# The narrow feed-forward round moved from first to last, with all five wide down projections in seven products

## The reference, cut to what matters

```python
D_FF = ((8 * D_MODEL + 3 * 256 - 1) // (3 * 256)) * 256      # 2816
...
    h2 = rms_norm(x, norm2_g)
    ffn = (jax.nn.silu(h2 @ w_ffn_gate) * (h2 @ w_ffn_up)) @ w_ffn_down
    return x + ffn
...
    for l in range(DEPTH_2):          # 2 layers
        x = hybrid_layer(x, l, ...)
    return rms_norm(x, final_g)
```

## Time and profile before

| | |
|---|---|
| median of 3 runs | 2476.74 us (2476.72 to 2477.36) |
| profiled execution: time / span | 2478.95 / 2477.2 us |
| TensorE busy | 2441.6 us, 99% of the span, 11994 matmuls |
| VectorE busy | 1599.9 us, 65% |
| ScalarE busy | 1143.3 us, 46% |
| GpSimd busy | 196.1 us, 8% |
| granted TensorE clock, mean | 0.998 |

### The profile page before, as it was taken

How to read it: one execution, slowest core, us unless ns; L and a number is a source line. 1 busy time by engine, 2 the same in 40 slices (tenths; PEclk the granted TensorE clock), 3 DMA queues, 4 the chain that set the end, 5 groups by cost and what they waited for, 6 DMA issues and landing times.

```text
span 2477.2 us, 31952 instructions
## 1 busy us (share of the span) xinstructions
PE 2441.6 (99%) x11994; PEld 1984.8 (80%) x11994; DVE 1599.9 (65%) x2918; ACT 1143.3 (46%) x2011; POOL 196.1 (8%) x212
## 2 busy tenths in 40 slices
PE   8999999999999999999999999999999999999998
PEld 7888878788777787888888887887787887888887
DVE  6767668654657677546666686645558686556666
ACT  3437455333745656323333444336647473433333
POOL 0001000100000000002222000000000000022220
PEclk9999999999999999999999999999999999999999
DMA  5321223233323221233333242233233312333331
GB/s 153 87 76 31 86 78 119 61 89 103 85 74 94 88 89 55 72 116 102 102 102 102 61 145 67 71 94 114 60 94 84 88 64 85 98 124 101 96 101 69
DMA packets 118970, 221.70 MB, mean 89 GB/s; under 512 B 14353, under 2 KB 21825, under 8 KB 118305
## 3 DMA queue, kind: packets, MB, share of 16 engines
q1 hardware_dynamic: 114192, 201.60, 26.9%
q0 software_dynamic: 4480, 17.79, 2.5%
q10 hardware_dynamic: 144, 0.26, 0.0%
HBM read 215.40 MB, written 4.23 MB: 89 GB/s over the span
## 4 chain that ended last, share of the span: by engine, by line
PE 91%; DVE 4%; ACT 3%; issue 2%; DMA 0%; SPq 0%; ACTq 0%; DVEq 0%
PE bank L749 52%; PE bank L746 21%; PE bank L805 6%; PE bank L929 2%; PE bank L940 2%; PE bank L1006 1%; PE bank L905 1%; PE bank L906 1%; PE bank L955 1%; PE bank L990 1%; PE bank L1044 1%; PE bank L823 0%; DVE tab L2019 0%; DVE hL L1928 0%; PE bank L837 0%
## 5 line engine op out<-in xcount | busy, mean ns | idle before, releaser
L1825 DVE TENSOR_TENSOR wL<-wraw,wH 128x1024 fp32r<-128x1024 f32 (+2 forms) x356 | 446.3, 1254 | 569.2 <-ACT wH L1223 567.3
L1223 ACT ACTIVATE wH<-wraw 128x1024 fp32r<-128x1024 f32 (+2 forms) x356 | 364.7, 1024 | 859.2 <-PE bank L749 633.2
L749 PE MATMUL bank<-hH,wH 128*128 128x512 f32 x1704 | 686.0, 403 | 1.8 <-ACT hH L1297 0.9
L749 PE MATMUL bank<-hH,wL 128*128 128x512 f32 x1704 | 666.3, 391 | 0.0
L749 PE MATMUL bank<-hL,wH 128*128 128x512 f32 x1704 | 665.8, 391 | 0.0
L749 PEld LDWEIGHTS bank<-hH,wH 128*128 128x128 f32 x1704 | 320.5, 188 | 76.1 <-issue 11.1
L749 PEld LDWEIGHTS bank<-hL,wH 128*128 128x128 f32 x1704 | 320.6, 188 | 72.3 <-issue 7.7
L749 PEld LDWEIGHTS bank<-hH,wL 128*128 128x128 f32 x1704 | 320.3, 188 | 70.1
L746 PE MATMUL bank<-wH,hH 128*128 128x512 f32 (+2 forms) x736 | 281.8, 383 | 0.0
L746 PE MATMUL bank<-wL,hH 128*128 128x512 f32 (+2 forms) x736 | 276.9, 376 | 0.0
L746 PE MATMUL bank<-wH,hL 128*128 128x512 f32 (+2 forms) x736 | 276.8, 376 | 0.0
(11 more groups left out here) (365 smaller groups left out, 3447.6 us busy)
## 6 DMA issues: line engine op xcount, KB each, us to landing
wraw<-in_w_in_dram SPq DMA_DIRECT2D x180, 512.0 KB, 3.6
wraw<-in_w_ffn_gate_dram SPq DMA_DIRECT2D x40, 512.0 KB, 3.7
wraw<-in_w_ffn_up_dram SPq DMA_DIRECT2D x40, 512.0 KB, 3.6
set<-in_w_ffn_down_dram SPq DMA_DIRECT2D x32, 512.0 KB, 6.1
wraw<-in_w_out_dram SPq DMA_DIRECT2D x24, 512.0 KB, 3.5
wraw<-in_w_ffn_down_dram SPq DMA_DIRECT2D x12, 512.0 KB, 3.5
wraw<-in_w_up_a_dram SPq DMA_DIRECT2D x8, 512.0 KB, 3.5
wraw<-in_w_up_b_dram SPq DMA_DIRECT2D x8, 512.0 KB, 3.5
```

What stands on the lines that cost most here:

```text
L749: mm = pe.matmul(bank[b.bank0 + t][:, :], w_part[:, kk, t * P:(t + 1) * P], act_part[:, k, :], start=first, stop=last)
L1223: A(wH[:, u % W_SLOTS, 0:width], wraw[:, u % RAW_SLOTS, 0:width], ACT.Copy).then_inc(S["w_hi"], 1)
L1825: V.tensor_tensor(wL[:, u % W_SLOTS, 0:width], wraw[:, u % RAW_SLOTS, 0:width], wH[:, u % W_SLOTS, 0:width].bitcast(F32), ALU.subtract).th ...
```

## The change

The rounds are now five of 512 features and then one of 256. All five wide ones (0 to 4) have their down projection in seven products, beside the projections of rounds 1 to 5. FU0 uses banks 4 to 7, FU5 banks 2 and 3. FD50 and FD51 have two chunks of hidden features instead of four: FD50 one unit, FD51 two units of one chunk. The last norm's weight on the left halves is multiplied by GpSimd, and ScalarE's left output waits for it (`left_gained`).

```diff
@@ Block.__init__
-            self.units = [(k, 2) for k in order or range(0, kchunks, 2)]
+            width = 1 if by_tile and kchunks == 2 else 2
+            self.units = [(k, width) for k in order or range(0, kchunks, width)]
...
-FFN_COLS = [256] + [512] * 5
-SEVEN = (1, 2, 3, 4)
+FFN_COLS = [512] * 5 + [256]
+SEVEN = (0, 1, 2, 3, 4)
...
-                               bank0=n // P if f == 0 else 0)
+                               bank0=NT if f == 0 else n // P if n < SEQ else 0)
...
@@ gpsimd, behind the last round's sums
+            pool.wait_ge(S["gp_step"], 16 * 6)
+            for t in range(NT):
+                pool.wait_ge(S["half_ready"], 5 * NT + t + 1)
+                pool.tensor_tensor(x[:, t, LEFT], x[:, t, LEFT], final_g[:, LEFT], ALU.mult).then_inc(
+                    S["left_gained"], 1)
...
@@ scalar, left_out(t)
                     act.wait_ge(S["rstd_ready"], 5 * NT + 1 + t + 1)
+                    act.wait_ge(S["left_gained"], t + 1)
...
@@ vector, last_squares
-                    for t in range(NT if gain else 0):
-                        left = x[:, t, 0:SEQ]
-                        V.tensor_tensor(left, left, final_g[:, 0:SEQ], ALU.mult)
```

More of the change, by code:

```diff
@@ L158, in dense_plan @@
     units, groups = [], 0
-    used = [0] * (GATE_BANK + 1)
+    used = [0] * 8
     for b in blocks:
@@ L494, in build @@
         names = """
-            x_tile0 x_tile1 x_tile2 x_tile3 ident_norm consts masks_ready landed0 landed1 landed2 w_hi w_lo groups free0 free1 free2 free3 free4 free5
+            x_tile0 x_tile1 x_tile2 x_tile3 ident_norm consts masks_ready landed0 landed1 landed2 w_hi w_lo groups free0 free1 free2 free3 free4 free5 free6 free7 left_gained
             act_step dve_step gp_step
@@ L510, in build @@
         landed = [S["landed0"], S["landed1"], S["landed2"]]
-        free = [S[f"free{j}"] for j in range(GATE_BANK + 1)]
+        free = [S[f"free{j}"] for j in range(8)]
         block = ctx.enter_context(nc.Block())
@@ L1871, in left_rows, with last_squares @@
                     half_square(t, 0)
-            def last_squares(b, gain):
+            def last_squares(b):
                 def between(i):
@@ L2857, in _ @@
                         last_rows(L, name, right_out if L == DEPTH else xn_rows,
-                                  last_squares(B(ffn_order()[-2])[0], L == DEPTH))
+                                  last_squares(B(ffn_order()[-2])[0]))
                     elif name == ffn_order()[-2]:
```

## The result

The changed kernel took 2488.98 us (median of 6 runs, 2488.18 to 2490.98) against 2477.05 of the kernel before (6 runs, 2476.43 to 2478.57): a ratio of 1.0049, 95% interval 1.0038 to 1.0059, or 11.9 us more. Forecast were 5.7 more. TensorE's count fell as written (11994 to 11970 matmuls), and its share of the chain that ended last fell from 91 to 90%, while VectorE's rose from 4 to 5%.

A forecast was written before the change was run, and what follows sets the result against it. TensorE was taken to bound the kernel (91% of the chain), VectorE its very end. -4.15 + 2 x 1.4 + 3.94 + 3.13 = +5.7 us on 2476.74 gave 2482.5 us, range 2479.2 to 2486.0.

The forecast's parts named there:

- TensorE's count: Feed-forward part, both layers: twelve fewer down-projection matmuls per layer, -2.07 us each, -4.15 in all.
- FG0 and FU0 with 512 columns: First feed-forward round of each layer: starting with 512 columns brings no stall, 0 us.
- Product 0 of the narrow round: FG5/FU5: VectorE's weight subtraction waits for GpSimd's s2, ends behind product 0's due time; 1.4 us stall per layer.
- the worse case: Narrow round: VectorE's subtraction behind a 2.4 us GpSimd operation instead of a 1.29 one, stalling product 0 by 2.5 us.
- The end of layer 1: From FD50 to the next layer's AQ: VectorE's work nearly unchanged, giving back +3.94 us of the 10.88 taken off.
- of layer 2: From FD50 to the kernel's end: VectorE's list and collisions with GpSimd's multiplications give back +3.13 us of 10.88.
- the turn at a square: Layer 2's end: GpSimd's multiplication of row 0 holds VectorE's square of row 1 up by 0.55 us.
- the turn at the first scaling: Layer 2's end: GpSimd's multiplication of row 3 holds VectorE's first final scaling up by 0.4 us.
- Product 2's subtraction: Later in the narrow round: GpSimd's t4 done near 13.4 us, four us before product 2; no stall counted.
- rival 2: Narrow round falls further behind: products 2 and 3 delayed 0.5 to 1 us each, product 0 2.5; 2486, chance 0.10.
- rival 1: Fewer collisions: product 0 waits 0.45 us, last stage has none; +2.9, 2479.6, chance 0.27 including what lies between.

The follow-up runs named there:

- early weights: Changed kernel with product 0's weights in the narrow round FG5 copied by ScalarE and subtracted by VectorE one unit earlier: 2480.43 us, ratio 1.0014.

## Why the prediction was wrong

- *TensorE's count, -4.15*: right. 24 matmuls fewer, and from FG0's plain run to the first products it is 51.7 us in layer 2 where it was 2205.91 - 2121.35 = 84.6: 32.8 less, forecast 32.64.
- *FG0 and FU0 with 512 columns, 0*: right. That run stands in the chain without a break.
- *Product 0 of the narrow round, +1.4 a layer*: this is the step that failed. It measured 3.2. The mechanism, turns with GpSimd, was right, and I had a price for the worse case: "with a 2.4 us GpSimd operation in front instead of a 1.29, 2.5". But I took the order of two instructions from a schedule in which they stood 0.1 us apart, and treated it as given. They came 0.04 us apart, the other way round. And even that bound was 0.7 low, since it had only the subtraction wait, not the split ahead of it as well. Two layers: 3.6 us.
- *TensorE's clock*: had no term. The early weights win 8.5 us, and 6.4 of them are the waits; the falls behind them, with the slower restart, account for the other 2 (1.8 in the profile). The feed-forward part of the kernel before has no wait and no such fall, but its trace has one elsewhere, in the block of the first kind, which the forecast left out. TensorE waits 3.0 us and goes on at 318.16 (the wait, and the window behind it, columns as above):

```profile
PE bank L837 <- DVE merged L1891: 3.0, 1, 3.0
...
318.00:322.00 4.00, 3.61 (x15) 0.57 0.12 11
```

- *The end of layer 1, +3.94, and of layer 2, +3.13*: right to 0.2 us (4.12 and 3.12), the turn at a square included. In layer 2 it is partly luck: the turn at the first scaling was 0.2 us less than I had, and row 0's add came 0.1 later.
- *Product 2's subtraction*, which I let pass, took 3.10 us instead of 1.2 in layer 1, and product 2's 12 matmuls 3.00 instead of 2.76. In layer 2 they took 1.21 and 2.76. Small, but of rival 2's kind; that the one delays the other no run shows.

With 1.8 more a layer and 1.8 for the clock the sum is +5.7 + 3.6 + 1.8 = 11.1. The slower restart of layer 1 and product 2 add 0.5 and give the 11.6 of the two cut stretches; the medians differ by 11.9. Rival 2 (2486) had the right sign and place and was still short. By its own terms, 1.1 and 1 to 2 us more a layer than the forecast, it should have read 2486.7 to 2488.7, so the range ended too low; at its other end 2479.2 stands for rival 1's 2479.6. I gave rival 2 0.10, when half my forecast's price hung on 0.1 us.

## What to carry to other kernels

Where VectorE runs instructions with two SBUF inputs beside GpSimd's work on SBUF, a hand-made schedule must be priced in both orders when they ask within some tenths of a microsecond of each other, and the range must reach to the worse. The cheap cure is to move the one instruction that TensorE waits for a unit earlier: here 8.5 us for a few lines. And a saving in TensorE's count is worth only what the engines behind it can follow: 24 matmuls fewer gave 4.2 us, and the two ends took 7.2 back, since VectorE's adds there no longer waited for TensorE.

## What the runs showed of the hardware

A wait of 3.2 us in an otherwise busy TensorE stream cost its own length and some 0.3 us in the 12 matmuls behind it. Behind 5 of 8 such waits the granted clock also fell, to a mean of 0.57 to 0.79 over the 8 us that begin about there, and the matmuls took 1.3 to 2.8 us more. Behind waits of 1.8 to 1.9 us it fell in two of three cases (0.72 over 6 us). Where s2 asked 0.02 to 0.04 us ahead of the split, VectorE's split took 1.1 us longer, in all 8 cases. A VectorE square of 0.69 us took 1.25 beside a GpSimd multiplication.
